# A hybrid decoder layer on one core: the output projection's chunks multiplied in two halves of the tokens

## What is computed

```
h      = rmsnorm(x) * (1 + sc1) + sh1
z      = h @ w_in + b_in                      # s5, mlstm, fox inputs and three gates
merged = g_s5 * (y_s5 @ w_up_s5) + g_m * (y_m @ w_up_mlstm) + g_f * (y_f @ w_up_fox)
x      = x + g1 * (merged @ w_out)            # the output projection
h      = rmsnorm(x) * (1 + sc2) + sh2
x      = x + g2 * ((silu(h @ w1) * (h @ w3)) @ w2)
out    = rmsnorm(x) * final_g
```

## Time and profile before

| | |
|---|---|
| median of 3 runs | 876.93 us (875.0 to 878.51) |
| the profiled execution's own time | 872.08 us |
| its span, first to last instruction | 870.3 us |
| PE busy | 847.0 us (97%) |
| mean granted clock of PE | 0.995 |
| instructions | 10546 |

### The profile page before, as it was taken

The page is one execution under the profiler, slowest core; times in us unless marked ns, Lnnn a source line. Parts: engine busy times, 40 slices in busy tenths (PEclk is TensorE's granted clock), DMA queues, the critical chain, the costliest instruction groups (busy, mean ns, idle before and its releaser), DMA issues.

```text
span 870.3 us, 10546 instructions
## 1 busy us (share of the span) xinstructions
PE 847.0 (97%) x3932; PEld 681.4 (78%) x3932; DVE 438.8 (50%) x703; ACT 323.8 (37%) x478; POOL 48.2 (6%) x75
## 2 busy tenths in 40 slices
PE   5999999999999999999999999999999999999996
PEld 3578888877787777787888778888888888888886
DVE  6789877247778654225873453333333333323222
ACT  4535445442323444343333553333333332222231
POOL 5310000000000000000001110000000000000110
PEclk9899999999999999999999999999999999999999
DMA  9833223348775121114234223333333333333322
GB/s 357 264 77 104 72 73 90 79 145 289 253 256 170 49 73 49 49 49 169 74 97 121 73 73 96 96 96 96 96 96 96 96 96 91 105 96 90 103 72 96
DMA packets 149372, 100.67 MB, mean 116 GB/s; under 512 B 11072, under 2 KB 142552, under 8 KB 148312
## 3 DMA queue, kind: packets, MB, share of 16 engines
q1 hardware_dynamic: 149128, 100.14, 37.9%
q10 hardware_dynamic: 208, 0.05, 0.0%
HBM read 97.03 MB, written 2.10 MB: 114 GB/s over the span
## 4 chain that ended last, share of the span: by engine, by line
PE 87%; DVE 5%; DMA 3%; ACT 2%; issue 1%; SPq 1%; DVEq 0%; ACTq 0%
PE bank L1696 25%; PE bank L1698 25%; PE bank L1697 25%; DMA raw<-in_w_in 3%; PE bank L1913 2%; PE bank L1843 1%; PE bank L1935 1%; PE bank L1863 1%; PE bank L1874 1%; DVE wlo L1190 1%; PE bank L1960 1%; ACT whi L696 1%; PE bank L1926 1%; PE bank L1911 1%; PE bank L1815 0%
## 5 line engine op out<-in xcount | busy, mean ns | idle before, releaser
L1696 PE MATMUL bank<-h_lo,whi 128*128 128x512 f32 x712 | 285.9, 402 | 1.8 <-DVE wlo L1190 1.0
L1698 PE MATMUL bank<-h_hi,wlo 128*128 128x512 f32 x712 | 278.1, 391 | 0.0
L1697 PE MATMUL bank<-h_hi,whi 128*128 128x512 f32 x712 | 277.9, 390 | 0.0
L1696 PEld LDWEIGHTS bank<-h_lo,whi 128*128 128x128 f32 x712 | 134.2, 189 | 32.2 <-issue 3.7
L1697 PEld LDWEIGHTS bank<-h_hi,whi 128*128 128x128 f32 x712 | 134.3, 189 | 28.7 <-issue 1.7
L1698 PEld LDWEIGHTS bank<-h_hi,wlo 128*128 128x128 f32 x712 | 134.1, 188 | 28.8
L1190 DVE TENSOR_TENSOR wlo<-raw,whi 128x1024 fp32r<-128x1024 f32 x60 | 73.3, 1223 | 104.7 <-ACT whi L696 104.7
L696 ACT ACTIVATE whi<-raw 128x1024 fp32r<-128x1024 f32 x60 | 63.2, 1055 | 151.3 <-PE bank L1698 107.8
L1698 PE MATMUL bank<-a_hi,wlo 128*128 128x512 f32 x176 | 68.5, 389 | 0.0
L1696 PE MATMUL bank<-a_lo,whi 128*128 128x512 f32 x176 | 68.5, 389 | 0.0
L1697 PE MATMUL bank<-a_hi,whi 128*128 128x512 f32 x176 | 68.5, 389 | 0.0
(11 more groups left out here) (334 smaller groups left out, 1005.8 us busy)
## 6 DMA issues: line engine op xcount, KB each, us to landing
raw<-in_ffn_w SPq DMA_DIRECT2D x60, 512.0 KB, 3.8
raw<-in_w_in SPq DMA_DIRECT2D x44, 512.0 KB, 4.0
slab<-in_mod_w SPq DMA_DIRECT2D x32, 512.0 KB, 5.9
modA<-in_mod_w SPq DMA_DIRECT2D x4, 1024.0 KB, 10.9
modB<-in_mod_w SPq DMA_DIRECT2D x4, 1024.0 KB, 18.4
raw<-in_w_out SPq DMA_DIRECT2D x8, 512.0 KB, 3.7
raw<-in_ffn_w SPq DMA_DIRECT2D x8, 384.0 KB, 3.2
xtok<-in_x SPq DMA_DIRECT2D x4, 512.0 KB, 5.6
```

Source lines behind the costliest of these rows:

```text
L1696: mm(dst, w_h, m_l, start=first, stop=False)
L1697: mm(dst, w_h, m_h, start=False, stop=False)
L1698: return mm(dst, w_l, m_h, start=False, stop=last)
```

## The change

Each of the eight chunks of the output projection is multiplied in two passes over k, first for tokens 0 to 255 and then for tokens 256 to 511, each half into its own half of the PSUM bank. A chunk is then 48 records of 256 columns, each with its weight load, in place of 24 records of 512. In chunk 0 the waits for `m_lo` stand in the first half, before each of its eight blocks; `x_again(7)` and the wait for `s_up` stand before block 6 of the second half. In chunk 7 `square_columns` stands before block 6 of the second half.

```diff
-                for k in range(KB):
-                    if n == 0 and k == KB - 2:
+                for k in range(2 * KB):
+                    half, k = divmod(k, KB)
+                    if n == 0 and half and k == KB - 2:
                         x_again(KB - 1)
                         pe.wait_ge(s_up, 3 * KB)
-                    if n == KB - 1 and k == KB - 2:
+                    if n == KB - 1 and half and k == KB - 2:
                         pe.wait_ge(s_x2c, KB)
                         pe.wait_ge(s_sqa, KB - 2)
                         square_columns(sqa, True)
-                    if n == 0:
+                    if n == 0 and half == 0:
                         pe.wait_ge(s_mlo, k + 1)
-                    ins = split_mm(ps[n % 2][:], whi[:, s % 3, k], wlo[:, s % 4, k], m_hi[:, k], m_lo[:, k],
+                    c = slice(256 * half, 256 * half + 256)
+                    ins = split_mm(ps[n % 2][:, c], whi[:, s % 3, k], wlo[:, s % 4, k], m_hi[:, k, c], m_lo[:, k, c],
                                    k == 0, k == KB - 1)
                 ins.then_inc(w_mm, 1)
```

## The result

The changed kernel took 883.08 us (median of 12 runs, 877.87 to 884.7) beside 874.77 us for the kernel before (12 runs on the same chip). The ratio is 1.0079, 95% interval 1.0055 to 1.0103: slower by 6.9 us, between 4.8 and 9.0. The medians are 8.3 us apart; the ratio goes by all the fast runs and leaves out one slow run of the kernel before, of 953.35 us. I had forecast +3.7 us, +0.42%, with 0.46 on a loss of over 0.5%.

A forecast was written before the change was run, and what follows sets the result against it. PE's record spacing was taken as the bound, except chunk 0's wait on VectorE's `m_lo`; 2.8 us for the gap plus 0.9 for spacing gave +3.7 us on the 876.93 median, 880.6 us, range 878.4 to 885.0.

The forecast's parts named there:

- Step 1: Chunk 0: PE waits 3.1 us for late `m_lo` in place of 0.45, so chunk 1 starts 2.8 us later.
- Step 2: Chunks 1 to 7: 336 half records at 0.116 us in place of 168 at 0.2267, +0.9 us.
- The guess about the refilling queue: Half records in chunks 1 to 7: PE's queue would hardly ever fill up, so 0.116 us a record was taken.
- The floor from the earlier trace: Half records: a weight load with its product can be issued every 0.112 us, the lower bound on spacing.
- Step 3: Weight splits, chunk 0's residual and chunk 7's column sums stay hidden; short waits at chunk starts 0 to 0.1 us each.
- Rival A: Gap in chunk 0: the clock falls to half, losing 1.7 to 3.4 us, sum +5.4 to +7.1; chance 0.24.
- one fall: Trace of the kernel before: the clock fell once, to 0.50 for 6.85 us from 32.0 on, and waits passed without one.
- Rival B: Half records: weight loads or issue bind at 0.121 us or more, sum +5.6 us and up; chance 0.16.

The follow-up runs named there:

- experiment 4: The change with six filler products on PE in the gap before block 6 of chunk 0's first half: ratio 1.0055, chunk 0 with its transposes 9.89 us.
- Experiment 3: The change with chunk 0 doing blocks 0 to 5 of both halves, then transposes, then blocks 6 and 7 of both: ratio 1.0042, chunk 0 7.30 us.
- experiment 1: The kernel before with chunk 0 left whole and chunks 1 to 7 halved: ratio 1.004, 0.1200 us a record.
- experiment 6: The kernel before with chunk 0 whole and chunks 1 to 7 in quarters of 128 columns: ratio 1.041, 0.1116 us a record.
- experiment 2: The kernel before with only chunk 0 halved, in the order of the change: ratio 1.0064, chunk 0 with its transposes 11.38 us.
- experiment 9: The kernel before with weight loads of 64 of 128 columns in chunks 1 to 7, leaving out half their output channels: 0.2300 us a record.

## Why the prediction was partly right

**What bounds the kernel.** Right: chunk 0 hangs on VectorE's late `m_lo` at a time that PE doesn't set, the rest on PE's spacing, and what is lost there arrives whole at the end (behind it 378.7 us against 378.6).

**Step 1, the gap.** Right in mechanism and size. Forecast: a wait of 3.1 us from the end of the first records, +2.8 us. Measured: 2.79 us idle (2.95 from when a next record could have started, which is how the forecast counted), and +2.80 where the clock is held up (experiment 4). Experiment 3 shows that the order makes it.

**Step 2, the spacing.** The mechanism was named, the size was wrong: +0.9 forecast, +2.18 measured, and the 0.1200 of a record lies above the 0.113 to 0.119 that the forecast gave as its sign. The reason is that I let the surplus go by columns. It goes by records: 0.0133 us on 512 columns and on 256 (experiment 1), 168 records more, 2.2 us. What misled me was the choice between two rows. The distance of the fillers in the earlier trace rows said per record, the lengths of the forget rows' products in the earlier trace rows said per column, and I took the latter, though the end of a PE record is modelled in this profile and the distance of starts is measured. The guess about the refilling queue went the wrong way too: just behind the transposes half records came 0.117 apart (451.02 to 451.49 is four starts, 0.47 / 4), and 0.120 once the stream ran. The floor from the earlier trace rows, 0.112, holds (experiment 6). By the rule of the Trainium skill, "TensorE: Matmul & The Clock Gate", section "Back-to-back issue gap", which its table gives for a product by itself, step 2 would have been +0.4 us, an estimate. The runs disagree, in that the fixed time of these records, each with its load, is 0.0133 us and not the few cycles stated.

**Step 3** held: PE was busy through all 41.20 us of chunks 1 to 7, so nothing there made it wait.

**Rival A, the clock.** It had 0.24 and came: two profiles show it, and as all 12 runs of the change and all 9 of experiment 2 have a mean clock of 0.993 or less, I take it to come in every execution. I was misled by the end of the kernel before, where the clock stayed up through most of 4 us with no work. The window behind that one shows that the clock did fall there, so the row was no proof that a pause leaves it alone, and the prediction's "one fall" was a misreading:

```profile
868.00:870.30 2.30, 0.00 (x0) 0.00 (x0) 0.00 (x0) 0.00 (x0) 0.00 (x0) 0.50 0.63 248
```

The price was less than the 1.7 to 3.4 us put on it: 1.03 us in the change (experiment 4 against it), 1.49 in experiment 2. The falls lasted 3.41 us, the lower end of what was allowed for, and in the change 0.54 us of it lay on the wait. And at half clock a half record took 0.2133 us, its columns with no surplus: in experiment 2, 16 of them in 3.40 us, against 16 x 0.1200 = 1.92, lose about 1.5, as measured. The Trainium skill, "TensorE: Matmul & The Clock Gate", section "Why this matters for your kernels", warns of idle gaps between bursts of products; the two profiled runs with a wait of 2.8 us agree with the warning.

**Rival B** was half right: 0.120 was at the edge of its 0.121, but the bound is not the floor of a pair of load and product, which is at 0.1116 (experiment 6), and the surplus doesn't go by the load's columns (experiment 9).

**The sum.** 2.80 for the gap, 1.03 for the clock, 2.18 for the records: +6.0 us between the profiled stages, within the measured 4.8 to 9.0. The forecast of 3.7 lacked the clock and 1.3 us of step 2. That the range, 878.4 to 885.0, held the median of 883.08 is in part luck: rival A came together with most of B's price, and the prediction said that its range leaves out A with B together. It held because the fall cost less than was put on it; and the kernel before took 874.77 us in these runs, not the 876.93 from which the range was counted (the 8.3 us between the medians, added to that, would end at 885.2).

## What to carry to other kernels

Before a loop over k is split and its halves are run one behind the other, look for what arrives late in k: the first pass has to wait for it with half of the work as cover, and the second pass, which needs nothing late, stands behind it; put the late blocks last in both. Splitting float32r products that each have their own weight load doubles a fixed 0.0133 us a record, and under some 236 columns (an estimate: 0.1116 less 0.0133 us at 2.4 GHz) the floor of a pair sets the pace, at 0.112 us. A wait on PE of nearly 3 us can cost its own length and then a stretch at half clock; in these runs half as long a wait, or fillers, kept the clock.

## What the runs showed of the hardware that I had not expected

The surplus of a float32r record with its own weight load, 0.0133 us over its columns at 2.4 GHz, is the same on 512 and 256 columns, whether the record adds in PSUM or overwrites, and whether or not the one before used the same columns and weights; the float32 fillers, with 512 passes, carry only 0.216 - 0.213 = 0.003. At 1.2 GHz the half records carried none, 0.2133 us for 256 columns. A weight load of half the columns made whole records slower, 0.2300 against 0.2267. What the surplus is was not found; a fixed time of each weight load was not tested.

With an idle stretch of 2.8 us in chunk 0 the clock fell in both profiled runs, once 0.54 us before the wait's end and once 0.6 us after it, when PE was already working again; it stayed up in the profiled runs with 1.49 and 0.19.
